# Constants, the first norm and the first projection of a trunk layer in one stage

## What is computed

```python
a = rmsnorm(h, norm_mix)                    # (1152, 1024)
z = a @ w_in                                # (1024, 9240), split into q, k, v, gates of two mixers
h = h + (sig(g_m)*(mLSTM(z)@w_br_m) + sig(g_f)*(attention(z)@w_br_f)) @ w_out
h = h + peer(rmsnorm(h, norm_ffn))          # 128 of 16384 single-neuron experts for each token
h = h + sigmoid(rmsnorm(h, norm_ple) @ w_ple_gate) * (p @ w_ple_proj)
y = rmsnorm(h, norm_final)
```

## Time and profile before

| | us |
|---|---|
| median of three runs | 5355.18 |
| lowest, highest | 5352.43, 5361.35 |
| the profiled execution | 5363.01 |
| its span, first to last instruction | 5361.3 |
| start of the first x load | 9.61 |
| start of the projection's matmuls | 90.24 |
| start of the next stage | 592.94 |

### The profile page before, as it was taken

The page is one execution under the profiler, slowest core; times in us unless marked ns, Lnnn a source line. Parts: engine busy times, 40 slices in busy tenths (PEclk is TensorE's granted clock), DMA queues, the critical chain, the costliest instruction groups (busy, mean ns, idle before and its releaser), DMA issues. The chain is left out here.

```text
span 5361.3 us, 47933 instructions
## 1 busy us (share of the span) xinstructions
PE 4561.7 (85%) x16510; PEld 2798.1 (52%) x16510; DVE 3077.7 (57%) x6238; ACT 990.3 (18%) x1824; POOL 1241.5 (23%) x970
## 2 busy tenths in 40 slices
PE   4999687978959999767788688946899999999989
PEld 2555464545645555455666555635455544545434
DVE  1000142312785776678888706689677777777742
ACT  2000241111110111144444311103100000000013
POOL 0000000110003444333333200000344444444410
PEclk9999887989979999877666699979999999999999
DMA  2333225448729999988888697725899999999951
GB/s 93 121 109 121 86 68 185 169 155 312 264 86 379 407 406 403 360 290 317 315 335 309 232 343 255 274 85 213 315 418 419 419 417 414 415 408 415 417 225 61
DMA packets 464562, 1478.72 MB, mean 276 GB/s; under 512 B 38290, under 2 KB 204994, under 8 KB 361442
## 3 DMA queue, kind: packets, MB, share of 16 engines
q0 software_dynamic: 119872, 824.76, 38.1%
q1 hardware_dynamic: 344482, 651.36, 33.9%
HBM read 1370.06 MB, written 115.38 MB: 277 GB/s over the span
## 5 line engine op out<-in xcount | busy, mean ns | idle before, releaser
L2125 POOL DMA_INDIRECT ex_uv<-in_uv,idx x768 | 1153.1, 1501 | 1892.6 <-DVE ex_acc L2182 1639.8
L2166 DVE CUSTOM_DVE_ANT_0 ex_uv<-ex_uv,ex_xp 128x1024 f32<-128x1024 f32 x768 | 916.0, 1222 | 352.1 <-DMA ex_uv<-in_uv,idx 302.0
L2182 DVE SCALAR_TENSOR_TENSOR ex_acc<-ex_uv,ex_wt,ex_acc 128x1024 f32<-128x1024 f32 x768 | 942.3, 1280 | 6.8 <-DVE ex_wt L2173 0.3
L2472 PE MATMUL exp_psum_dn<-exp_dn_big,exp_dn_gg 128*128 128x512 f32 x1536 | 686.6, 597 | 27.5 <-DVE exp_dn_gg L2394 27.4
L2463 PE MATMUL exp_psum_dn<-exp_dn_xT,exp_dn_big 128*128 128x384 f32 x2048 | 684.2, 488 | 13.3 <-DMA exp_dn_big<-in_ud 13.3
L259 PE MATMUL proj_psum_acc<-proj_w,aT_later 128*128 128x385 f32 x1920 | 626.5, 488 | 69.0 <-DMA proj_w<-in_w_in 66.7
L2463 PEld LDWEIGHTS exp_psum_dn<-exp_dn_xT,exp_dn_big 128*128 128x128 f32 x2048 | 390.5, 191 | 313.4 <-issue 62.5
L259 PEld LDWEIGHTS proj_psum_acc<-proj_w,aT_later 128*128 128x128 f32 x1920 | 365.1, 190 | 329.9 <-DMA proj_w<-in_w_in 66.9
L259 PE MATMUL proj_psum_acc<-proj_w,aT 128*128 128x385 f32 x1536 | 499.4, 487 | 8.9 <-DMA proj_w<-in_w_in 8.9
L2472 PEld LDWEIGHTS exp_psum_dn<-exp_dn_big,exp_dn_gg 128*128 128x128 f32 x1536 | 291.5, 191 | 378.7 <-issue 351.7
L259 PEld LDWEIGHTS proj_psum_acc<-proj_w,aT 128*128 128x128 f32 x1536 | 291.3, 190 | 216.9 <-DMA proj_w<-in_w_in 9.3
(11 more groups left out here) (363 smaller groups left out, 4559.7 us busy)
## 6 DMA issues: line engine op xcount, KB each, us to landing
proj_w<-in_w_in SPq DMA_DIRECT2D x48, 1540.0 KB, 8.9
rt_w<-in_w_q SPq DMA_DIRECT2D x36, 2048.0 KB, 8.2
exp_dn_big<-in_ud SPq DMA_DIRECT2D x128, 512.0 KB
exp_dn_big<-in_vd SPq DMA_DIRECT2D x128, 512.0 KB
scratch_z<-proj_zs SPq DMA_DIRECT2D x216, 192.5 KB
rt_w<-in_w_br_m SPq DMA_DIRECT2D x18, 2048.0 KB, 10.1
rt_w<-in_w_br_f SPq DMA_DIRECT2D x18, 2048.0 KB
rt_w<-in_w_out SPq DMA_DIRECT2D x18, 2048.0 KB, 9.3
```

The lines of the kernel that those rows point to most:

```text
L2125: pool.indirect_dma_start(self.uv[:, slot, :], None, self.uv_tab, bass.IndirectOffsetOnAxis(ap=self.idx[:, at:at + 1], axis=0)).then_inc(s ...
L2166: dve.tensor_tensor_reduce(self.uv[:, slot, 0:D], self.uv[:, slot, 0:D], self.xp[:], 1.0, 0.0, ALU.mult, ALU.add, self.dot[:, g % 2, j:j + ...
L2182: dve.scalar_tensor_tensor(out=self.acc[:, j % 2, :], in0=self.uv[:, slot, D:2 * D], scalar=self.wt[:, g % 2, j:j + 1], in1=self.acc[:, j ...
L2472: mm = pe.matmul(self.banks[t][:, n * 512:(n + 1) * 512], self.gg[:, 4 + q % 4, t * P:(t + 1) * P], self.big[:, 4 + q % 4, n * 512:(n + 1) ...
```

## The change

`stage_constants`, both `stage_norm` and the first `stage_project` become one stage, `stage_front`.

- SyncE issues the x load of tile 0, the gain, the x loads of tiles 1 to 3, and right behind them the first three weight chunks. The x loads of tiles 4 to 8 come at steps 0, 12, 24, 36 and 48.
- GpSimd makes the identity first, with a semaphore of its own; the other tables follow.
- The sum of squares moves from ScalarE to VectorE (`tensor_tensor_reduce`). Four x buffers, two `xn` buffers, two half-tile PSUM banks in place of one tile of two banks. The gain is applied by two VectorE operations of 128x512.
- TensorE turns tile t (0 to 3) just before step t and waits until VectorE has stored both halves. Tiles 4 to 8 are turned ahead of steps 12, 24, 36, 48 and 60, with no wait for their store.
- The projection has six PSUM banks and six output buffers in place of five. Its steps, their order and the weight chunks stay as they are.
- The second `stage_project` and all that follows are untouched.

```diff
-def stage_constants(nc, K):
...
-def stage_norm(nc, K, x, g_cols, aT, t0, nt):
...
+class Constants:
...
+    def pool(self, pool):
+        K = self.K
+        pool.memset(K["ident"][:], 0.0).then_inc(self.filled, 1)
+        pool.wait_ge(self.filled, 1)
+        n = 1
...
+        cut_to(K["ident"], flat, [[-1, P]], 0, 1, ALU.not_equal, 1.0, self.ident_cut)
...
+    def pe_first(self, pe):
+        pe.wait_ge(self.ident_cut, 1)
+    def dve_last(self, dve):
+        dve.wait_ge(self.cut, 4)
+        dve.tensor_reduce(self.K["masknew"][:], self.K["bmask"][:].rearrange("p (n j) -> p j n", n=NSEQ), AX.X,
+                          ALU.max).then_inc(self.reduced, 1)
+        dve.wait_ge(self.reduced, 1)
+class Norm:
+    XB = 4
+    def __init__(self, K, st, x, g_cols, nt, dest):
+        self.K, self.x, self.g_cols, self.nt, self.dest = K, x, g_cols, nt, dest
+        self.xt, self.xn, self.sq = st.sb("xt", [P, self.XB, D]), st.sb("xn", [P, 2, D]), st.sb("sq", [P, D])
+        self.gain = st.sb("gain", [P, KD])
+        self.ss, self.ms, self.rt, self.rs = (st.sb(n, [P, 2]) for n in ("ss", "ms", "rt", "rs"))
+        self.half = [st.ps(f"half{h}", [P, 512]) for h in range(2)]
+        self.gain_in, self.squared, self.meaned, self.rooted, self.inverted, self.normed, self.turned, self.stored = (
+            st.sems("gain_in squared meaned rooted inverted normed turned stored"))
+        self.x_in = [st.sem(f"x_in{s}") for s in range(self.XB)]
+    def sp_gain(self, sp):
+        sp.dma_start(self.gain[:], self.g_cols).then_inc(self.gain_in, 16)
+    def sp_load(self, sp, i):
+        if i >= self.XB:
+            sp.wait_ge(self.normed, i - self.XB + 1)
+        sp.dma_start(self.xt[:, i % self.XB], self.x[i * P:(i + 1) * P, :]).then_inc(self.x_in[i % self.XB], 16)
+    def dve_mean(self, dve, i):
+        s = i % 2
+        dve.wait_ge(self.x_in[i % self.XB], (i // self.XB + 1) * 16)
+        xt = self.xt[:, i % self.XB]
+        dve.tensor_tensor_reduce(self.sq[:], xt, xt, 1.0, 0.0, ALU.mult, ALU.add, self.ss[:, s:s + 1]
+                                 ).then_inc(self.squared, 1)
+        dve.wait_ge(self.squared, i + 1)
+        if i >= 2:
+            dve.wait_ge(self.rooted, i - 1)
+        dve.tensor_scalar(self.ms[:, s:s + 1], self.ss[:, s:s + 1], 1.0 / D, EPS, ALU.mult, ALU.add
+                          ).then_inc(self.meaned, 1)
+    def act_root(self, act, i):
+        s = i % 2
+        act.wait_ge(self.meaned, i + 1)
+        if i >= 2:
+            act.wait_ge(self.inverted, i - 1)
+        act.activation(self.rt[:, s:s + 1], self.ms[:, s:s + 1], ACT.Sqrt).then_inc(self.rooted, 1)
+    def dve_invert(self, dve, i):
+        s = i % 2
+        dve.wait_ge(self.rooted, i + 1)
+        if i >= 2:
+            dve.wait_ge(self.normed, i - 1)
+        dve.reciprocal(self.rs[:, s:s + 1], self.rt[:, s:s + 1]).then_inc(self.inverted, 1)
+    def act_scale(self, act, i):
+        s = i % 2
+        act.wait_ge(self.inverted, i + 1)
+        if i >= 2:
+            act.wait_ge(self.turned, 2 * i - 2)
+        act.activation(self.xn[:, s], self.xt[:, i % self.XB], ACT.Copy, scale=self.rs[:, s:s + 1]
+                       ).then_inc(self.normed, 1)
+    def pe_turn(self, pe, i):
+        pe.wait_ge(self.normed, i + 1)
+        for h in range(2):
+            if i >= 1:
+                pe.wait_ge(self.stored, 2 * i + h - 1)
+            for k in range(4):
+                at = (4 * h + k) * P
+                mm = pe.transpose(self.half[h][:, k * P:(k + 1) * P], self.xn[:, i % 2, at:at + P], self.K["ident"][:])
+            mm.then_inc(self.turned, 1)
+    def dve_store(self, dve, i):
+        if i == 0:
+            dve.wait_ge(self.gain_in, 16)
+        aT, c = self.dest(i)
+        for h in range(2):
+            dve.wait_ge(self.turned, 2 * i + h + 1)
+            dve.tensor_tensor(aT[:, 4 * h:4 * h + 4, c * P:(c + 1) * P],
+                              self.half[h][:].rearrange("p (k t) -> p k t", k=4),
+                              bc(self.gain[:, 4 * h:4 * h + 4], [P, 4, P]), ALU.mult).then_inc(self.stored, 1)
+def stage_front(nc, K, x, g_cols, aT, aT_later, w_in, z):
+    with Stage(nc, "proj0") as st:
+        U, nt = 3, FIRST
+        STEPS = CHUNKS * nt
+        SLOTS = 6
+        w = st.sb("w", [P, U, KD, CW])
+        zs = st.sb("zs", [P, SLOTS, CW])
+        cn = Constants(K, st)
+        nm = Norm(K, st, x, g_cols, NT, lambda i: (aT, i) if i < nt else (aT_later, i - nt))
+        acc = [st.ps(f"acc{s}", [P, 512]) for s in range(SLOTS)]
+        summed, read = st.sems("summed read")
+        w_in_u = [st.sem(f"w_in{u}") for u in range(U)]
+        out = [st.sem(f"out{s}") for s in range(SLOTS)]
+        w_in_v = w_in.rearrange("(k p) n -> p k n", p=P)
+        rides = {(i - nt + 1) * 3 * nt: i for i in range(nt, NT)}
+        @block.sync
+        def _(sp):
+            def load(u):
+                if u >= U:
+                    sp.wait_ge(summed, (u - U + 1) * nt)
+                sp.dma_start(w[:, u % U], w_in_v[:, :, u * CW:(u + 1) * CW]).then_inc(w_in_u[u % U], 16)
+            nm.sp_load(sp, 0)
+            nm.sp_gain(sp)
+            for i in range(1, nm.XB):
+                nm.sp_load(sp, i)
+            for u in range(U):
+                load(u)
+            for j in range(STEPS):
+                u, t = divmod(j, nt)
+                if j + 3 * nt in rides:
+                    nm.sp_load(sp, rides[j + 3 * nt])
+                sp.wait_ge(read, j + 1)
+                sp.dma_start(z[t * P:(t + 1) * P, u * CW:(u + 1) * CW], zs[:, j % SLOTS, :]
+                             ).then_inc(out[j % SLOTS], 16)
+                if t == nt - 1 and u + U < CHUNKS:
+                    load(u + U)
+            for s in range(SLOTS):
+                sp.wait_ge(out[s], (STEPS - s + SLOTS - 1) // SLOTS * 16)
         @block.gpsimd
         def _(pool):
+            cn.pool(pool)
+        @block.tensor
+        def _(pe):
+            cn.pe_first(pe)
+            for j in range(STEPS):
+                u, t = divmod(j, nt)
+                if u == 0:
+                    nm.pe_turn(pe, t)
+                    pe.wait_ge(nm.stored, 2 * t + 2)
+                if j in rides:
+                    nm.pe_turn(pe, rides[j])
+                if t == 0:
+                    pe.wait_ge(w_in_u[u % U], (u // U + 1) * 16)
+                if j >= SLOTS:
+                    pe.wait_ge(read, j - SLOTS + 1)
+                for k in range(KD):
+                    mm = pe.matmul(acc[j % SLOTS][:, 0:CW], aT[:, k, t * P:(t + 1) * P], w[:, u % U, k, :],
+                                   start=(k == 0), stop=(k == KD - 1))
+                mm.then_inc(summed, 1)
+        @block.scalar
+        def _(act):
+            for i in range(nt):
+                nm.act_root(act, i)
+                nm.act_scale(act, i)
+            for j in range(STEPS):
+                act.wait_ge(summed, j + 1)
+                if j >= SLOTS:
+                    act.wait_ge(out[j % SLOTS], j // SLOTS * 16)
+                act.copy(zs[:, j % SLOTS, :], acc[j % SLOTS][:, 0:CW]).then_inc(read, 1)
+                if j + nt in rides:
+                    nm.act_root(act, rides[j + nt])
+                if j + nt - 1 in rides:
+                    nm.act_scale(act, rides[j + nt - 1])
         @block.vector
         def _(dve):
+            nm.dve_mean(dve, 0)
+            for i in range(nt):
+                if i + 1 < nt:
+                    nm.dve_mean(dve, i + 1)
+                nm.dve_invert(dve, i)
+                if i >= 1:
+                    nm.dve_store(dve, i - 1)
+            nm.dve_store(dve, nt - 1)
+            cn.dve_last(dve)
+            for i in range(nt, NT):
+                nm.dve_mean(dve, i)
+                nm.dve_invert(dve, i)
+                nm.dve_store(dve, i)
...
-        stage_constants(nc, K)
...
-            stage_norm(nc, K, A["x"], A["norm_mix"], aT_later, FIRST, NT - FIRST)
...
-                stage_norm(nc, K, A["x"], A["norm_mix"], aT, 0, FIRST)
-                stage_project(nc, aT, A["w_in"], z, 0, FIRST)
+                stage_front(nc, K, A["x"], A["norm_mix"], aT, aT_later, A["w_in"], z)
```

More of the change, by code:

```diff
@@ new lines, in _ @@
+            for s in range(SLOTS):
+                sp.wait_ge(out[s], (STEPS - s + SLOTS - 1) // SLOTS * 16)
+        @block.gpsimd
+        def _(pool):
+            cn.pool(pool)
[17 more added lines that the diff above has]
+                mm.then_inc(summed, 1)
@@ L172, in _ @@
         @block.scalar
         def _(act):
[L174 to L181, removed]
@@ L183, in _ @@
-        @block.tensor
-        def _(pe):
-            with pe.Fori(0, nt) as i:
-                pe.wait_ge(normed, i + 1)
-                pe.wait_ge(stored, i)
-                for k in range(KD):
-                    mm = pe.transpose(tp[:, k * P:(k + 1) * P], xn[:, k * P:(k + 1) * P], K["ident"][:])
-                mm.then_inc(turned, 1)
+            for i in range(nt):
```

(13 more changed lines are left out.)

41 lines of the change are left out of this document (34 added, 7 removed).

## The result

The changed kernel takes 5291.24 us (median of four runs, 5288.23 to 5296.66), the kernel before 5358.27 beside it: a ratio of 0.9879, with a 95% interval of 0.9866 to 0.9891. That is 67 us less, where 66.8 were forecast, and the time, 2.8 us above the forecast of 5288.4, lies inside the range. The profiled execution took 5289.55 us.

The account below looks back on a forecast made before the run. The projection was taken as bound by its matmuls, the norm stages before it as idle. 12.6 + 6.87 + 6.3 + 492.6 + 4.5 = 522.9 us for the last copy against 589.68, so 5355.2 - 66.8 = 5288.4 us, range 5279 to 5303.

Parts of the forecast that it names:

- Start of the matmuls: Start of the merged stage: norm of tile 0 ready at 11.6 us, weights end the wait, matmuls start at 12.6.
- First step: First projection step, from first matmul to first copy: 6.87 us as before, the clock taken as cold again.
- rival B: TensorE's eight new stops: the clock falls, each costs 1.69 us, 13.5 us in all; time 5301.9; chance 0.06.
- Tiles 1 to 3: Before steps 1 to 3 TensorE turns a tile and waits for both stores: 2.1 us each, 6.3 in all.
- Tiles 4 to 8: Turns within the stream of projection steps: 0.9 us of TensorE each, 4.5 in all.
- The other steps: Remaining projection steps, copy to copy: 95 x 5.185 us = 492.6 us.
- SyncE, ScalarE and the constants: Their loads, copies, scales and tables beside the projection: cost nothing while it is bound by matmuls.
- The profiled execution: Whole profiled run: 5363.0 us becomes 5296.2, 66.8 less; the earlier one lay 7.8 above the median.
- A, weights later by sharing: Start: three weight chunks share the DMA engines, matmuls start at 20.7 us, 8.1 later; time 5296.5; chance 0.10.
- C, half clock that stays: Projection steps: clock stays at half, steps take 10.4 us, 13 such use up the gain; slower than before; chance 0.02.
- The bound for VectorE held up by GpSimd: Start: tile 0's mean begins only when GpSimd's selects end, 7.6 for 4.4; matmuls 2.2 us later; not taken.

Follow-up runs that it names:

- the kernel with the weights second: Changed kernel with the first weight chunk right behind x of tile 0 and the gain, and each tile stored before the next is summed: 5290.91 us.
- the second trace: The changed kernel once more, unchanged, in five rounds against the kernel before: median 5289.98 us, ratio 0.9865.
- gaps of 4.40: Changed kernel with TensorE also waiting at the five turned tiles among the steps for two stores and three dead VectorE fills: 5319.82 us.

## Why the prediction held

The gain forecast was 66.8 us, the medians give 67.0, the means 65.4, the front alone 64.4 (the first two traces) to 66.1 (the means). The mechanism was right; that the medians meet the forecast within 0.2 us is luck, since whole times scatter by 5.7 and the front gave 0.7 to 2.4 us less than forecast. Term by term:

**Start of the matmuls.** Forecast 12.6, measured 14.49 and 13.65: this is the term that was mis-sized. That the weights end the wait was right (the wait of 2.2 us), and that they come behind x is shown by the kernel with the weights second. Two things make them later than reckoned. One is the rate. I took 385 GB/s, from a microsecond of weight loads, for x as well. The changed kernel's stretches show less while x is moving, in the first trace all the time (the last two columns are DMA share and GB/s), in the second for one microsecond:

```profile
3.00:4.00 1.00, 0.00 (x0) 0.00 (x0) 0.00 (x0) 0.00 (x0) 0.85 (x7) 1.00 0.76 269
...
6.00:7.00 1.00, 0.00 (x0) 0.00 (x0) 0.01 (x1) 0.20 (x1) 1.00 (x5) 1.00 1.02 295
...
11.00:12.00 1.00, 1.00 (x6) 0.87 (x5) 0.47 (x1) 0.82 (x2) 0.00 (x0) 1.00 1.06 393
```
```profile
5.00:6.00 1.00, 0.00 (x0) 0.00 (x0) 0.92 (x3) 0.01 (x1) 1.00 (x2) 1.00 0.79 172
...
7.00:8.00 1.00, 0.00 (x0) 0.00 (x0) 0.72 (x4) 0.21 (x1) 1.00 (x4) 1.00 1.04 410
```

The other is that the chunks overlap. The packets up to 12.92 us and up to the start at 14.49 in the changed kernel, and up to the start at 90.24 in the kernel before:

```profile
DMA packets 1752, 3.68 MB, mean 285 GB/s; under 512 B 216, under 2 KB 1240, under 8 KB 1752
...
DMA packets 2144, 4.27 MB, mean 295 GB/s; under 512 B 224, under 2 KB 1632, under 8 KB 2144
```
```profile
DMA packets 1231, 1.87 MB, mean 258 GB/s; under 512 B 16, under 2 KB 1231, under 8 KB 1231
```

At 12.92 as many chunk packets had moved as the first chunk has (1240 - 216 = 1,024), yet the wait went on for 1.6 us, and by its end 1,408 had moved, 384 of them of the chunk behind. In the second trace it is 1.15 us (12.50 to 13.65) and 281 packets, in the kernel before 0.8 us (89.46 to 90.24) and 191. So of the miss of 1.9 and 1.05 us some 0.8 and 0.4 are a longer overlap of the chunks than in the kernel before, and 1.1 and 0.7 the slower x (estimates from these rows).

Tile 1's x came at 7.52 in the first trace and between 5.97 and 7.76 in the others with this order of loads (6.26 in the second), for 5.8 in the forecast, and with it the norm was ready at 13.0 (11.8 in the second), not 11.6; but the weights were later still.

**First step.** Forecast 6.87, as before, counted to the copy. Counted to the next transposes it is 7.36 (21.85 - 14.49) and 6.67, and the copy would follow 0.2 us later (21.03 and 21.23 where each tile is turned one ahead): 7.56 and 6.87. In the other new traces it lies between 6.7 and 8.3 to the transposes. (Of the 1.69 us that rival B takes for a cold start, some 0.3 belong to any step behind a gap: 5.49 from first matmul to copy where a step in the stream takes 5.185.) So the time at half clock at the start differs from run to run.

**Tiles 1 to 3.** Forecast 2.1 us each; the copies of steps 2 and 3 are 7.27 apart, 7.27 - 5.185 = 2.09. **Tiles 4 to 8.** Forecast 0.9 each; 6.06 - 5.185 = 0.88, at all five. **The other steps** 5.18. **SyncE, ScalarE and the constants** at nothing: no wait of TensorE for any of them after the start, and the distances of the copies show no other irregularity.

The sum of 522.9 for the last copy was 525.25 and 523.71, late by 0.8 to 2.4, and the last copy of before scatters by 1.4 in the other direction (589.68 to 591.07), so that the two nearly cancel in the gain.

**The profiled execution.** Forecast 5296.2 from 5363.0; it took 5289.55. The 6.6 us between are 9.4 less behind the front (4759.0 against 4768.4, where the execution of before that was profiled had the longest such part of three), less the 2.5 by which the front gained less than forecast. I had put it at 7.8 above the median and had rightly not carried that into the forecast of the median.

**The rivals.** A, weights later by sharing: its price, a start of 20.7, is refuted by 14.49 and 13.65; the mechanism exists in part, as the 384 and 281 packets of the next chunk show. B, clock falls at the gaps: the mechanism exists (1.7 and 2.8 us behind gaps of 4.40), but not at 0.95 us, as the gap of 1.68 in the earlier trace rows said. The Trainium skill's "TensorE: Matmul & The Clock Gate", in the section named in the prediction, says that bursts with idle gaps between them fall back to half clock; the trace agrees for the gaps of 4.40 us (granted clock 0.50 behind them), and not for those of 0.95. C, half clock that stays: the step behind each long gap is whole again, refuted. The bound for VectorE held up by GpSimd (2.2 us) was not used; the Trainium skill's rule in "SBUF — State Buffer", section "Who interferes with whom", that the two exclude each other, is borne out by the selects of 1.10 to 1.32 us, and here it was mostly GpSimd that waited.

## What to carry over

When a program starts with stages that leave every engine mostly idle in front of one that is bound by a single engine, merging them is worth the distance between the first instruction and the bound engine's start, and it can be forecast to a few microseconds by rebuilding that one start: what lands first on the shared DMA queue, at which rate, and how far the loads behind it overlap with it. Work that must go onto the bound engine itself costs its warm price in the stream (0.88 us here, under half of the 1.94 to 1.97 that it shows when it stands alone), plus any wait between it and its consumer; turning one step ahead took that wait away. A gain of 5 us in 5290 can be read from landmarks in the trace, but with this scatter behind it not from the time.

## What was not expected

- One instruction's mutual exclusion is dear to the short side: a 0.29 us select on GpSimd took 1.10 to 1.32 us when it met a 1.22 us sum of two SBUF operands on VectorE, which itself lost 0.0 to 0.25 us.
- The same 4.40 us of idleness on TensorE cost the following step 1.7 us at three places and 2.8 at two.
- The same x loads of 512 KB moved at 269 to 330 GB/s from 3 to 8 us in one trace of the changed kernel, and at 172 to 410 in the other, where the weight loads behind them moved at 370 to 395 in both. What makes the start of the queue uneven was not tried.
- A load is not alone on the queue until it has landed: one packet of the first chunk was outstanding while 130 of the x loads behind it had moved.
